# The norm's bias on the residual rows: sixteen half rows on GpSimd, or eight full rows on ScalarE inside the next projection

## The chip, the cores and the metric

The kernel runs on one core of a Trainium2 chip. The metric is the device time of one execution in microseconds; the median of three runs of the kernel before is 2121.49 us (2120.16 to 2122.59).

## What is computed

The reference is one inference step of a decoder trunk with two layers, for 512 prompt positions and 8 x 8 sample positions (576 columns in all) and a model width of 1024, in float32:

```python
for l in range(DEPTH):                      # DEPTH = 2
    mix, caches = token_mixer(x, ...)       # pooling, latent attention, gated MLP; from one projection w_in
    x = layernorm(ALPHA * x + mix, ln1_g[l], ln1_b[l])
    ffn, tail = conv_ffn(x, ...)            # w_up, 3-tap convolution, silu(gate) * up, w_down
    x = layernorm(ALPHA * x + ffn, ln2_g[l], ln2_b[l])

def layernorm(x, g, b):
    mu = mean(x); xc = x - mu
    return xc * rsqrt(mean(xc * xc) + LN_EPS) * g + b
```

So there are four norms, n = 0 to 3: two in layer 0 and two in layer 1. The result of a norm goes to two places: into the next projection, and, multiplied by ALPHA, into the next residual sum. The change is about the second.

## The kernel before

**Layout.** Features lie on the 128 partitions, positions in the free dimension. The residual X is a tile of eight rows (k = 0 to 7, one for each 128 features) of 576 columns. A half row is 288 of them. For TensorE every float32 operand is split into a high part (fp32r) and the remainder: X into XH and XL, a weight unit WS into WH (ScalarE copies, helper line 548) and WL (VectorE subtracts, line 1434). Each product takes three matmuls: WH XH, WH XL, WL XH. A tile of 128 output features takes 8 x 3 matmuls for one half of the columns and 48 for both (line 1010).

**Order.** There is no scheduler: each engine's program is written out by hand, and semaphores that only count up tie them together. Weight units (512 KB, or 704 KB for the down projection) are fetched by SP through two main slots; a slot's next fetch waits until VectorE has made the unit's remainder (w_lo). TensorE waits for w_lo and for the PSUM pair (mm_free0 or mm_free1) that ScalarE or VectorE releases once it has read it.

**A norm.** The projection before a norm (w_out or the second half of w_down) is done in two passes over the columns. While the second pass runs, the first half of the columns is normalised. The second half is normalised while TensorE already runs six tiles of the next projection on the first half (`first_halves`). The steps of a half, by line: VectorE centres (1451), ScalarE squares (574), TensorE sums through a matrix of ones (1052 to 1070), ScalarE takes the root (579), VectorE the reciprocal (1461) and then, for each row k, the scaled row X[k] = X[k] * gain * 1/sigma (1468, semaphore n_xn). ScalarE writes XH[k] = X[k] + bias (593, semaphore n_hi), and VectorE the remainder XL[k] = X[k] + bias - XH[k] (1479, semaphore n_lo). Both read X without the bias. So X itself gets the bias only after n_lo of its row: GpSimd does it, in `add_bias` (lines 491 to 495), one half row after another, and counts n_x. In the second half the order on ScalarE is: weight copy, XH rows 0 and 1, rows 2 to 4, the eviction of the fifth tile (which releases mm_free0), rows 5 to 7, the eviction of the sixth.

**After norms 0 and 2** comes the up projection: 11 tile pairs j = 0 to 10 in each of two halves hf, a gate tile (par 0) and an up tile (par 1) each. For j = 0, 2 and 4 of hf = 0 the six tiles of `first_halves` have already made the first half of the columns (kept in STASH), so that only 24 matmuls a tile are left; the other pairs take 48 a tile. In `up_tile` ScalarE copies the state (SFT) and the tile into EB, then makes a weight's high part, and for the gate tile runs silu when VectorE's convolution taps (1963, 1970, 1976) are done; last it copies HX to HH. The Silu table is loaded at line 938, ahead of j = 0. On VectorE a weight's remainder stands behind the taps of the gate tile (except for the half tiles, where it stands after the first tap), and for the up tile behind the product of silu and up. VectorE waits for n_x ahead of the first down projection (line 2006).

**After norm 1** comes layer 1's combined projection w_in: six tiles a of `first_halves` on the first half, then tiles m = 0 to 11, of which 0 to 4 and 10 have only the second half left (24 matmuls). For each m ScalarE waits for the tile, copies a weight's high part, evicts the tile into Z and releases its PSUM pair. Between the tiles it also loads w_uk, w_ukt and w_uv, and at m = 3 squares the v rows (line 691), which TensorE sums behind tile 4 (line 1041). X is overwritten by gathered cache pages during the attention, so after norm 1 the biased X is saved to x_save in DRAM by GpSimd's queue (line 513), in four transfers of 576 KB, each behind four of the adds. The first gather of layer 1 (line 535), into the space of X, waits for all four.

Norm 3 is the last; its bias is added by ScalarE on the way to the output, and nothing changes there.

Of the kernel before, what the change touches and what calls it, by code (L numbers as in the profile page):

```python
# [106 lines left out]
def build(nc, x_t, x_save, cache_wide, page_table, branch_in, w_uk, w_ukt, w_uv, state_ffn_t, params,  # L107
# [3 lines left out]
    with ctx:  # L111
# [353 lines left out]
        @block.gpsimd  # L465
        def _(pool):
            for name, n in CREDIT.items():
                pool.sem_inc(S[name], n)

            def norm(l, n, m0):  # L470

                def sum_up(half, k):
                    u = 8 * half + k
                    pool.wait_ge(S[f"mm_free{u % 2}"], CREDIT[f"mm_free{u % 2}"] + l * NM + m0 + u // 2 + 1)
                    if k == 0:
                        return
                    h = half_of(half)
                    pool.tensor_tensor(XS[:, h], X[:, 0, h] if k == 1 else XS[:, h], X[:, k, h], ALU.add)  # L478
                    ins = pool.drain()
                    if k == (DT - 1, DT - 2)[half]:  # L480
                        ins.then_inc(S["n_xs"], 1)

                def sum_squares(half, k):
                    pool.wait_ge(S["n_sq"], ln(n, half, k + 1))
                    h = half_of(half)
                    pool.tensor_tensor(SS[:, h], LSQ[:, 0, h] if k == 1 else SS[:, h], LSQ[:, k, h], ALU.add)
                    ins = pool.drain()
                    if k == (DT - 1, DT - 3)[half]:
                        ins.then_inc(S["n_sqs"], 1)

                def add_bias(half, k):
                    pool.wait_ge(S["n_lo"], ln(n + 1, half, k + 1))
                    h = half_of(half)
                    pool.tensor_scalar(X[:, k, h], X[:, k, h], param(l, (C_1B, C_2B)[n % 2] + k), None, ALU.add)\
                        .then_inc(S["n_x"], 1)

                last = n == 2 * DEPTH - 1
                for k in range(DT):
                    sum_up(0, k)
                for k in range(1, DT):  # L500
                    sum_squares(0, k)
                for k in range(DT - 1):
                    sum_up(1, k)
                if not last:
                    for k in range(1, DT - 2):
                        sum_squares(1, k)
                    for half in range(2):
                        for k in range(DT):
                            add_bias(half, k)
                            if n % 2 == 1 and k % 4 == 3:  # L510
                                pool.wait_ge(S["n_x"], ln(n, half, k + 1))
                                ks = slice(k - 3, k + 1)
                                pool.dma_start(x_save[:, ks, half_of(half)], X[:, ks, half_of(half)])\
                                    .then_inc(S["x_saved"], 16)

            for l in range(DEPTH):
                for u in range(NU2):
                    b, j = u // 4, u % 4
                    if u == 0 and l == 0:
                        pool.wait_ge(S["mask"], 1)  # L520
                        pool.wait_ge(S["n_lo"], ln(0, 1))
                    if u == 0 and l > 0:
                        pool.wait_ge(S["x_saved"], 64 * l)
                    if u == 1:
                        pool.wait_ge(S["mm_done0"], CREDIT["mm_done0"] + l * NM + M_UQ + 2)
                        pool.wait_ge(S["w_lo"], l * NU + U_UQ + 2)
                    if u == 2:
                        for other in ("met_pe", "met_act", "met_dve"):
                            pool.wait_ge(S[other], l * N_MEET + 1)
                    if u >= 4:  # L530
                        pool.wait_ge(S["pv_mm"], CREDIT["pv_mm"] + l * NU2 + u - 3)
                    past(pool)
                    for q in range(NQ):
                        g = b * NG + NQ * j + q
                        pool.indirect_dma_start(  # L535
                            raw_of(u)[:, q, :], None, cache_wide.rearrange("l n c -> (l n) c"),
                            bass.IndirectOffsetOnAxis(ap=IDXS[:, l, g:g + 1], axis=0))\
                            .then_inc(S[f"g_landed{u % 4}"], 16)
                for n in range(4):
                    pool.wait_ge(S[f"g_landed{n}"], 16 * NQ * landings(l, NU2 - 4 + n))  # L540
                past(pool)
                norm(l, 2 * l, M_OUT)
                norm(l, 2 * l + 1, M_DOWN[1])

        @block.scalar
        def _(act):
# [34 lines left out]
            def normal_hi(n, half, ks):  # L581
                h, b0 = half_of(half), (C_1B, C_2B)[n % 2]
                for k in ks:
                    if n < 0:
                        act.wait_ge(S["x_in_b"], 32)
                        copy(XH[:, k, h], X[:, k, h]).then_inc(S["x_hi"], 1)
                        continue
                    act.wait_ge(S["n_xn"], ln(n, half, k + 1))
                    if n == 2 * DEPTH - 1:
                        nc.scalar.activation(X[:, k, h], X[:, k, h], ACT.Identity,  # L590
                                             bias=param(n // 2, b0 + k)).then_inc(S["n_x"], 1)
                    else:
                        nc.scalar.activation(XH[:, k, h], X[:, k, h], ACT.Identity,
                                             bias=param(n // 2, b0 + k)).then_inc(S["n_hi"], 1)

            def half_passes(l, n, u0, m0, width):

# [53 lines left out]
            for l in range(DEPTH):  # L651
# [24 lines left out]
                for m in range(12):  # L676
# [4 lines left out]
                    if m < 11:  # L681
                        weight_hi(l * NU + U_IN + m + 2, D if m < 10 else QT * 384)
                        if z_of[m] is not None:
                            evict(m)
                            act.wait_ge(S["z_ev"], l * 16 + 6 + (m + 1 if m < 5 else m - 1))
                            act.sem_inc(S[f"mm_free{m % 2}"], 1)
                    if m == 3:
                        if l == 0:
                            act.wait_ge(S["params"], 16)
                        act.wait_ge(S["v_centred"], l + 1)  # L690
                        nc.scalar.activation(SQV[:, :, :], Z[:, 8:10, :], ACT.Square).then_inc(S["v_sq"], 1)
# [277 lines left out]
                for hf in range(2):  # L969
                    first = 2 * len(UP_FIRST) if hf == 0 else 0  # L970
                    for j in range(first):
                        up_tile(hf, j, D, UP_FIRST.index(j) if j in UP_FIRST else None)
                    with act.Fori(first, FH - 1) as j:
                        up_tile(hf, j, D)
                    up_tile(hf, FH - 1, UW, last=hf == 1)
# [1209 lines left out]
```

## Time and profile before

| | |
|---|---|
| median of the runs | 2121.49 us |
| profiled execution, first to last instruction (its only time) | 2123.8 us |
| TensorE matmul / weight load busy | 2047.8 / 1891.6 us |
| VectorE / ScalarE / GpSimd busy | 1194.9 / 804.0 / 401.2 us |
| mean granted TensorE clock | 0.994 |

Busy time is the time in which an engine had an instruction under way. An idle time in brackets behind a row is that of its engine just before the row, with what ended it. "Issue" there stands for a release that the profile does not show. In rows that merge several instructions, xN gives their number. Times in rows are microseconds from the start of the span, the mean duration in groups is in nanoseconds. The granted clock is given as a share of full speed; 1.00 is 2.4 GHz and 0.50 is 1.2 GHz.

### The profile page before, as it was taken

To read this page: it belongs to the slowest core of one execution; us is meant where nothing else is said; L and a number is where in the kernel's file an instruction comes from. 1 tells how busy PE (TensorE), PEld (TensorE's weight loads), DVE (VectorE), ACT (ScalarE), POOL (GpSimd) and SP (SyncE) were. 2 spreads that over 40 slices of the span, in tenths; PEclk is the share of its full clock that TensorE was granted. 3 is DMA by queue.
4 is the path that set the end of the run, shared out by engine and by line. 5 is a ranking of instruction groups with operands and counts; after the bars stand their busy time and mean duration, and the time that the engine had idled before them with its cause. 6 is when DMAs were issued, how large, how long until landed. Compare 5 with 4: busy or idle time off the path is not lost.

```text
span 2123.8 us, 43041 instructions
## 1 busy us (share of the span) xinstructions
PE 2047.8 (96%) x17374; PEld 1891.6 (89%) x17374; DVE 1194.9 (56%) x2032; ACT 804.0 (38%) x1508; POOL 401.2 (19%) x407
## 2 busy tenths in 40 slices
PE   7999999999998999999999999999999999999997
PEld 7976667999998999999989766689999889999997
DVE  4764545333578652666758644453335876436665
ACT  4343434222354321334443443342223543223334
POOL 0026661000051000000350366600002600000012
PEclk9999999999999999999999999999999999999999
DMA  7349996222433232225452599942225232222252
GB/s 253 118 149 328 373 353 232 80 79 80 156 108 96 84 105 67 79 79 181 136 206 68 174 364 365 370 161 88 80 79 175 90 100 79 99 71 82 79 195 73
DMA packets 88850, 325.69 MB, mean 153 GB/s; under 512 B 10576, under 2 KB 15568, under 8 KB 88592
## 3 DMA queue, kind: packets, MB, share of 16 engines
q1 hardware_dynamic: 46512, 169.52, 24.4%
q0 software_dynamic: 37440, 144.98, 18.4%
q10 hardware_dynamic: 4768, 9.37, 1.4%
q8 instruction: 92, 1.51, 0.3%
q14 instruction: 38, 0.31, 0.0%
HBM read 315.52 MB, written 7.26 MB: 152 GB/s over the span
## 4 chain that ended last, share of the span: by engine, by line
PE 84%; DVE 8%; ACT 3%; DMA 2%; issue 1%; DVEq 1%; POOL 0%; PEldq 0%; SPq 0%; ACTq 0%; PEld 0%; POOLq 0%
PE PS L1010 65%; PE PS L1292 5%; PE PS L1262 5%; DVE m_WL L1434 3%; PE PS L1283 2%; DMA m_WS<-in_w_units 1%; PE PS L1273 1%; ACT m_WH L548 1%; DVE m_X L1468 1%; PE PS L1315 1%; DVE m_XS L1479 1%; PE PS L1041 1%; PE PS L1331 1%; PE PS L1322 1%; PE PS L1309 1%
## 5 line engine op out<-in xcount | busy, mean ns | idle before, releaser
L1010 PE MATMUL PS<-m_XS,m_WH 128*128 128x288 f32 x5120 | 922.0, 297 | 34.6 <-DVE m_WL L1434 18.0
L1010 PEld LDWEIGHTS PS<-m_XS,m_WH 128*128 128x128 f32 x5120 | 767.9, 189 | 43.7 <-DVE m_WL L1434 20.9
L1010 PE MATMUL PS<-m_XS,m_WL 128*128 128x288 f32 x2560 | 583.5, 297 | 0.0
L1434 DVE TENSOR_TENSOR m_WL<-m_WS,m_WH 128x1024 fp32r<-128x1024 f32 (+2 forms) x284 | 369.2, 1301 | 229.9 <-ACT m_WH L548 221.0
L548 ACT ACTIVATE m_WH<-m_WS 128x1024 fp32r<-128x1024 f32 (+2 forms) x284 | 315.6, 1113 | 374.6 <-PE PS L1010 341.1
L1010 PEld LDWEIGHTS PS<-m_XS,m_WL 128*128 128x128 f32 x2560 | 423.5, 189 | 0.0
L535 POOL DMA_INDIRECT m_RAW<-in_cache_wide,m_IDXS x256 | 242.4, 947 | 380.2 <-PE PS L1010 124.4
L478 POOL TENSOR_TENSOR m_XS<-m_X 128x288 f32<-128x288 f32 x8 | 10.6, 1320 | 1170.5 <-DVE m_X L1488 1169.5
L1010 PE MATMUL PS<-m_HH,m_WH 128*128 128x288 f32 x704 | 205.7, 299 | 5.2 <-DVE m_X L1488 4.9
L1010 PE MATMUL PS<-m_HL,m_WH 128*128 128x288 f32 x704 | 203.5, 296 | 0.0
L1010 PE MATMUL PS<-m_HH,m_WL 128*128 128x288 f32 x704 | 180.3, 297 | 0.0
L1010 PEld LDWEIGHTS PS<-m_HH,m_WH 128*128 128x128 f32 x704 | 133.0, 189 | 6.3 <-DVE m_WL L1434 5.3
L1010 PEld LDWEIGHTS PS<-m_HL,m_WH 128*128 128x128 f32 x704 | 133.2, 189 | 0.2
L1292 PE MATMUL PS<-m_RAW,m_PT 128*64 128x256 f32 x1024 | 124.6, 385 | 7.4 <-ACT m_PT L548 7.1
L1262 PE MATMUL PS<-m_RAW,m_QSF 64*64 64x256 f32 x1024 | 125.3, 382 | 0.9 <-DMA m_RAW<-in_cache_wide,m_IDXS 0.9
L1262 PE MATMUL PS<-m_RAW,m_QSR 64*64 64x256 f32 x1024 | 124.4, 382 | 0.0
L1010 PEld LDWEIGHTS PS<-m_HH,m_WL 128*128 128x128 f32 x704 | 123.2, 189 | 0.0
L1963 DVE TENSOR_SCALAR m_CC<-m_EB,m_PARS 128x592 f32<-128x592 f32 x88 | 51.9, 590 | 123.5 <-ACT m_EB L548 123.4
L1292 PEld LDWEIGHTS PS<-m_RAW,m_PT 128*64 128x64 f32 x1024 | 67.8, 136 | 47.8 <-ACT m_PT L548 14.6
L902 ACT ACTIVATE m_SIG<-PS 128x576 f32<-128x576 f32 x48 | 31.2, 650 | 185.7 <-PE PS L1010 185.7
L1786 DVE TENSOR_SCALAR_CACHE_REDUCE PS<-PS,m_NMX 128x512 f32<-128x512 f32 x64 | 48.5, 759 | 92.0 <-PE PS L1273 92.0
L1262 PEld LDWEIGHTS PS<-m_RAW,m_QSF 64*64 64x64 f32 x1024 | 69.0, 133 | 28.0 <-issue 16.1
(276 smaller groups left out, 2875.4 us busy)
## 6 DMA issues: line engine op xcount, KB each, us to landing
m_WS<-in_w_units SPq DMA_DIRECT2D x232, 512.0 KB
m_WS<-in_w_units SPq DMA_DIRECT2D x48, 704.0 KB
m_RAW<-in_cache_wide,m_IDXS POOLq DMA_INDIRECT x256
m_X<-in_x_t SPq DMA_DIRECT2D x6, 576.0 KB, 7.4
m_WS<-in_w_units SPq DMA_DIRECT2D x4, 576.0 KB
x_save<-m_X POOLq DMA_DIRECT2D x4, 576.0 KB, 4.4
m_X<-x_save SPq DMA_DIRECT2D x4, 576.0 KB, 6.9
out_y<-m_X SPq DMA_DIRECT2D x8, 288.0 KB, 2.2
```

The lines of the kernel that those rows point to most:

```text
L535: pool.indirect_dma_start(raw_of(u)[:, q, :], None, cache_wide.rearrange("l n c -> (l n) c"), bass.IndirectOffsetOnAxis(ap=IDXS[:, l, g:g ...
L548: return nc.scalar.activation(out, in_, ACT.Copy)
L902: nc.scalar.activation(h2(SIG[:, g, :]), pair(g % 2), ACT.Sigmoid)\
L1010: mm = pe.matmul(out(half), w(part, k), x(k)[:, half_of(half)], start=(k == 0 and part == 0 and x is xh), stop=(k == last and part == 1))
L1041: mm = pe.matmul(PS[:, bank + h, 0:HT], C["ones"], x[:, h * HT:(h + 1) * HT], start=(k == 0), stop=(k == len(tiles) - 1))
L1262: pe.matmul(PS[64 * c:64 * c + 64, score_bank(u) + h, 0:256], weights, raw_of(u)[rows, c::2, at0:at0 + P], start=(g == 0), stop=False)
L1273: mm = pe.matmul(out[:, :, j, :], QSP[j][rows, rows_of], raw_of(u)[rows, c::2, 2 * KL:ROW], start=False, stop=(j == 1))
L1283: mm = pe.transpose(PS[:, 6, j * P:(j + 1) * P], PRB[:, j * P:(j + 1) * P], ident)
L1292: mm = pe.matmul(PS[64 * c:64 * c + 64, 7, 0:KL], PT[:, a, 64 * c:64 * c + 64], raw_of(u)[:, 2 * (a // 2) + c, j * KL:(j + 1) * KL], start ...
L1434: return dve.tensor_tensor(out, x, hi.bitcast(F32), ALU.subtract)
L1786: dve.tensor_scalar(s0, s0, -SCALE, NMX[:, b, j:j + 1], ALU.mult, ALU.min, accum_out=NMX[:, b, j + 1:j + 2]).then_inc(S["s_max"], 1)
L1963: dve.tensor_scalar(cc, e[:, 2:CV], tap(2), PARS[:, bass.ds(l * NPAR + C_CB + c, 1)], ALU.mult, ALU.add)
```

## The change

GpSimd's sixteen half-row adds of each of norms 0, 1 and 2 go. ScalarE adds the bias to eight full rows instead, as an Identity activation with the bias as its operand. It waits for the second half's n_lo of the row and counts n_x up by 2. After norms 0 and 2 it does rows 0 and 1 at the end of `up_tile` j = 2, rows 2 and 3 at the end of j = 3, and so on to j = 5. After norm 1 it does two rows at each of the tiles m = 0 to 3 of layer 1's combined projection, behind the eviction and the release of the PSUM pair. x_save is written in two transfers of 1152 KB, still from GpSimd's queue, each behind four full rows.

```diff
--- before.py
+++ after.py
@@ in gpsimd, norm() @@
-                def add_bias(half, k):
-                    pool.wait_ge(S["n_lo"], ln(n + 1, half, k + 1))
-                    h = half_of(half)
-                    pool.tensor_scalar(X[:, k, h], X[:, k, h], param(l, (C_1B, C_2B)[n % 2] + k), None, ALU.add)\
-                        .then_inc(S["n_x"], 1)
-
@@
-                    for half in range(2):
-                        for k in range(DT):
-                            add_bias(half, k)
-                            if n % 2 == 1 and k % 4 == 3:
-                                pool.wait_ge(S["n_x"], ln(n, half, k + 1))
-                                ks = slice(k - 3, k + 1)
-                                pool.dma_start(x_save[:, ks, half_of(half)], X[:, ks, half_of(half)])\
-                                    .then_inc(S["x_saved"], 16)
+                    if n % 2 == 1:
+                        for c in range(2):
+                            pool.wait_ge(S["n_x"], ln(n, 0, 0) + DT * (c + 1))
+                            ks = slice(4 * c, 4 * c + 4)
+                            pool.dma_start(x_save[:, ks, :], X[:, ks, :]).then_inc(S["x_saved"], 16)
@@
-                        pool.wait_ge(S["x_saved"], 64 * l)
+                        pool.wait_ge(S["x_saved"], 32 * l)
@@ in scalar @@
+            def add_bias(n, ks):
+                for k in ks:
+                    act.wait_ge(S["n_lo"], ln(n + 1, 1, k + 1))
+                    nc.scalar.activation(X[:, k, :], X[:, k, :], ACT.Identity,
+                                         bias=param(n // 2, (C_1B, C_2B)[n % 2] + k)).then_inc(S["n_x"], 2)
@@ in scalar, tiles m of the combined projection, behind the eviction @@
+                    if l > 0 and m < 4:
+                        add_bias(2 * l - 1, (2 * m, 2 * m + 1))
@@ in scalar, up projection @@
                     for j in range(first):
                         up_tile(hf, j, D, UP_FIRST.index(j) if j in UP_FIRST else None)
+                        if j >= 2:
+                            add_bias(2 * l, (2 * j - 4, 2 * j - 3))
```

## Rows read from the trace of the kernel before

**Rows 1.** The page, busy time, share of the span and instructions.
```profile
PE 2047.8 (96%) x17374; PEld 1891.6 (89%) x17374; DVE 1194.9 (56%) x2032; ACT 804.0 (38%) x1508; POOL 401.2 (19%) x407
```

**Rows 2.** The chain that ended last: the page's shares, and one piece in time.
```profile
PE 84%; DVE 8%; ACT 3%; DMA 2%; issue 1%; DVEq 1%; POOL 0%; PEldq 0%; SPq 0%; ACTq 0%; PEld 0%; POOLq 0%
...
644.42 16.12 PE PS L1010 x120
```

**Rows 3.** Timeline of TensorE: start, duration, instruction; in brackets idle before.
```profile
639.76 0.51 PE L1010 MATMUL PS<-m_XS,m_WH 128*128 128x288 f32 x2 [1.67 <-issue]
...
661.25 0.54 PE L1010 MATMUL PS<-m_XS,m_WH 128*128 128x288 f32 x2 [0.72 <-DVE m_WL L1434]
...
687.91 0.54 PE L1010 MATMUL PS<-m_XS,m_WH 128*128 128x288 f32 x2 [2.06 <-DVE m_WL L1434]
...
1082.94 0.82 PE L1010 MATMUL PS<-m_XS,m_WH 128*128 128x288 f32 x2 [3.59 <-issue]
```

**Rows 4.** Timeline of GpSimd at norms 0 and 1.
```profile
625.76 20.47 POOL L494 TENSOR_SCALAR m_X<-m_X,m_PARS 128x288 f32<-128x288 f32 x16 [0.22 <-issue]
...
1070.59 0.85 POOL L513 DMA_DIRECT2D x_save<-m_X  x1 [0.30 <-POOL m_X L494]
...
1085.05 4.80 POOL L494 TENSOR_SCALAR m_X<-m_X,m_PARS 128x288 f32<-128x288 f32 x4
```

**Rows 5.** Timeline of VectorE in the second half of norm 1.
```profile
1077.72 0.95 DVE L1479 SCALAR_TENSOR_TENSOR m_XS<-m_X,m_PARS,m_XS 128x288 fp32r<-128x288 f32 x2 [1.85 <-ACT m_XS L593]
...
1082.96 0.75 DVE L1479 SCALAR_TENSOR_TENSOR m_XS<-m_X,m_PARS,m_XS 128x288 fp32r<-128x288 f32 x1
...
1084.07 0.51 DVE L1479 SCALAR_TENSOR_TENSOR m_XS<-m_X,m_PARS,m_XS 128x288 fp32r<-128x288 f32 x1
```

**Rows 6.** Timeline of ScalarE, up projection of layer 0.
```profile
643.00 1.28 ACT L938 ACT_TABLE_LOAD   x1
...
677.50 0.20 ACT L548 ACTIVATE m_EB<-m_SFT 128x16 f32<-128x16 f32 x1
...
681.05 0.70 ACT L962 ACTIVATE m_SL<-m_CC 128x592 f32<-128x592 f32 x1 [1.81 <-DVEq L1979]
682.31 0.22 ACT L548 ACTIVATE m_EB<-m_SFT 128x16 f32<-128x16 f32 x1 [0.56 <-PE PS L1010]
...
687.35 0.20 ACT L548 ACTIVATE m_EB<-m_SFT 128x16 f32<-128x16 f32 x1
```

**Rows 7.** ScalarE's instructions by line: count, ns min/median/max, first and last start.
```profile
L702 ACT ACTIVATE m_Z<-m_Z,m_PARS x4: 852/854/857, 71.5 to 1123.6; 128x576 f32<-128x576 f32 x4
...
L593 ACT ACTIVATE m_XS<-m_X,m_PARS x48: 517/536/540, 605.9 to 1692.5; 128x288 fp32r<-128x288 f32 x48
```

**Rows 8.** Timeline of VectorE, weight remainders in the up projection.
```profile
681.10 1.23 DVE L1434 TENSOR_TENSOR m_WL<-m_WS,m_WH 128x1024 fp32r<-128x1024 f32 x1
...
702.93 1.22 DVE L1434 TENSOR_TENSOR m_WL<-m_WS,m_WH 128x1024 fp32r<-128x1024 f32 x1
```

**Rows 9.** Engines by stretch: length, busy each, granted clock, DMA share, GB/s.
```profile
688.00:692.00 4.00, 4.00 (x21) 4.00 (x22) 3.81 (x7) 1.18 (x3) 0.00 (x0) 0.63 0.53 147
...
1084.00:1088.00 4.00, 4.00 (x19) 4.00 (x18) 4.00 (x6) 1.37 (x3) 3.75 (x4) 0.50 0.44 155
...
1740.00:1744.00 4.00, 4.00 (x32) 4.00 (x32) 2.44 (x4) 1.41 (x6) 0.00 (x0) 1.00 0.64 229
```

**Rows 10.** The chain around norm 1: weight units, from request to landing.
```profile
1071.23 4.95 DMA m_WS<-in_w_units
...
1091.27 7.17 DMA m_WS<-in_w_units
```

**Rows 11.** Timelines of ScalarE and of TensorE: the v rows' square and its sum.
```profile
1102.26 1.17 ACT L691 ACTIVATE m_SQV<-m_Z 128x1152 f32<-128x1152 f32 x1
...
1104.22 2.10 PE L1041 MATMUL PS<-m_SQV,m_CST 128*128 128x288 f32 x8
```

## The prediction

> **What bounds the kernel now.** I read the page's engine shares first, then its chain, then TensorE's gaps in order of time, and last the queues of VectorE, ScalarE and GpSimd around the three places where the bias is added. The shares show a kernel that TensorE bounds nearly everywhere [rows 1], and the chain says the same; it holds stretches of 120 matmuls in 16.12 us, 0.134 us each [rows 2]. So a change on other engines counts only where TensorE stands still, or where it is made to. The reader is to see in [rows 3] that it stands still around every norm: 1.67 us at 639.76 and 0.72 at 661.25 behind norm 0, 2.06 at 687.91 in the up-projection, 3.59 at 1082.94 behind norm 1. Norm 2 repeats norm 0, 1050.3 us later. I call the up tiles j0, j1, ..., each a gate half (p0) and an up half (p1).
>
> GpSimd adds the sixteen half rows in one run, 20.47 us at norm 0, and at norm 1 in pieces between the x_save transfers, to 1089.85 [rows 4]. In just that time VectorE does the second half of the norm.
>
> **Part 1, sixteen adds leave GpSimd.** VectorE's remainder rows (L1479) show a price for them. At norm 1 one took 0.75 us while GpSimd worked, and the next one 0.51, while GpSimd, whose next adds start at 1085.05, was issuing a transfer [rows 4, 5]. So an overlapping add costs a remainder row 0.24 us. I take it from six remainder rows, and guess 0.34 in all for the scaled rows in the stretch: 1.8 us at norm 0 and again at norm 2, of which 1.5 lies before the last scaled row. Bounds: 0 (the slow ones are slow for another reason) and 16 x 0.24 = 3.8.
>
> The Trainium skill (SBUF — State Buffer, "Who interferes with whom") says that a VectorE instruction with two SBUF inputs contends with a GpSimd one that reads SBUF, and that one of the two blocks fully. Both VectorE forms here have two SBUF inputs; by that rule all sixteen would gain, 3.8 us, where the rows show a part of it. The sum goes by the rows.
>
> At norms 0 and 2 the last scaled row gates ScalarE's XH row 7, the sixth stash and then the table load, 1.28 us from 643.00 [rows 6]; they move 1.5 us earlier, and j0's copies with them. j0 and j1 are paced by ScalarE and VectorE (the 0.72 us gap at 661.25 ends on VectorE's weight split), so j2 starts 1.5 us earlier too: shift -1.5.
>
> **Part 2, eight full rows on ScalarE in j2 to j5 (norms 0 and 2).** A full row with a bias is not in this form in the trace. Below: the half row with a bias, 0.536 us; above: the full row with bias and scale, 0.854 [rows 7]. A pair costs 1.07 to 1.71; I take 1.35, a little under the middle, since rows in a row overlap. The Trainium skill (ScalarE: Activation LUTs, "What ACT_TABLE_LOAD costs") gives 280 ns + 0.833 ns per element for an activation with a bias operand and 93 ns of overlap; an estimate from that is 1.33 for a pair.
>
> The pair stands behind j's HH copy, ahead of the next tile's copies. Queued behind it: the copies of the gate half, behind these VectorE's taps and its weight split, and TensorE waits for the split.
> - After j2: ScalarE starts j3's copies at 677.50 with nothing idle before [rows 6]. New start: 677.50 - 1.5 + 1.35 = 677.35. The split for j4p0 ends 4.83 us later (681.10 + 1.23 - 677.50) [rows 8], at 682.2. TensorE, 1.5 us early, wants it at 680.8 (before, it came without a gap at 682.3): a new gap of 1.4 us.
> - j3p1's copies: ScalarE waited 0.56 us for TensorE there, to 682.31. Now silu is last, at 681.05 + 0.70 - 0.15, less 0.1 of overlap, 681.5: shift -0.8, and the split that ended the 2.06 us gap also comes 0.8 early, at 687.1.
> - After j3: 687.35 - 0.8 + 1.35 = 687.9, shift +0.55, carried rigidly through j4, where ScalarE never waits for TensorE. j5p0's weights come 0.7 us late for TensorE, which loses nothing more in the end, as the next line sets the time.
> - After j4: shift +0.55 + 1.35 = +1.9 at j5's copies. The split for j6p0 ended at 704.15 [rows 8]; now at 706.05. TensorE would be there at 687.1 + 0.7 + 16.1 (120 matmuls of 0.134) = 703.95: a gap of 2.1 us.
> - After j5: the pair ends before j6p0 does (6.4 us of TensorE); from here on TensorE bounds again, and nothing gives the delay back. VectorE's wait for n_x ahead of the first down projection costs nothing: the last pair ends near 712, and five more tile pairs of 12.9 us (j6 to j10) hide it.
>
> Before, TensorE began j6p0 16.1 us after 687.91 at norm 2's place (704.05), and 1.5 us later at norm 0, where the clock fell: 21 matmuls in four microseconds at 0.63 against 32 at 1.00 for the like tiles behind norm 2, 11 x 0.134 = 1.5 [rows 9]. So norm 0 costs +0.5 and norm 2 +2.0: +2.5. The shift at j5 is 2b - 0.8 with its own part of b in 0.8; with b from 1.07 to 1.71 the two together give +0.8 to +4.7.
>
> The clock: the same 2.06 us gap dropped it to 1.2 GHz at norm 0 and not at norm 2. The new 2.1 us gaps at j6p0 are of that size, one behind each norm. Half of them at 1.5 us, and a little for j4: +1.7 (bounds 0 and 3.5). Part 2 with what part 1 gives to it: **+4.2 us**.
>
> **Part 3, norm 1.** Two things end together: GpSimd's adds, and the four x_save transfers in the middle of the second half (one issued at 1070.59) [rows 4]. The weight unit requested at 1071.23 took 4.95 us to land and VectorE stood still for 1.85 us behind it [rows 5, 10], with its 512 KB beside a transfer of 576. Its share of the bytes is 2.3 us, the lower bound; I take 3.2. That gives 1.8 us, the scaled and remainder rows another 0.6 up to row 4, whose XH copy is ahead of the eviction that frees the PSUM pair: TensorE starts at about 1080.55, not 1082.94: -2.4. Its gap was 3.59 us and put the clock at 0.50: 19 matmuls in four microseconds, not 32, is 1.7 us [rows 9], and with what that stretch leaves out on both sides I take 2.3. The new gap is 1.6, like that of 639.76, behind which 120 matmuls ran at full pace [rows 2]. -4.7. The next tile's split waits for the last remainder row: +0.6.
>
> Then the pairs come, in tiles of half length (3.2 us): each 1.35 us behind the eviction and its release, so TensorE's tiles go on. Late is what ScalarE does after them: the square for v at 1102.26, which had its result 0.8 us before TensorE summed it at 1104.22 [rows 11]. Now the weight of tile 5 at 1096.0 (1.06), its eviction (0.3), the last pair (1.35) and the square (1.17) end at 1099.9, where TensorE would be at 1099.2. Net at this sum: 1104.3 - 1099.9 = **-4.4 us** (bounds -2.5 and -5.9, TensorE's own pace). Behind it full tiles of 6.4 us cover ScalarE. GpSimd's second transfer, twice the size, starts at about 1099, 9 us behind its last adds before, and the first gathers follow it; six such tiles and the whole query stage lie between them and the attention that reads them.
>
> **Sum.** +4.2 - 4.4 = -0.2. The page gives 2123.8 us as the span and no other time for its execution; the runs' median is 2121.49, 0.1% under it, so the difference is carried over: **2121.3 us**.
>
> **Rivals.**
> - *The pairs are hidden in the up-projection.* ScalarE is busy for 38% of the span only [rows 1], and the gap of 0.56 us before 682.31 is some cover. Against it: no idle time stands before 677.50 and 687.35 [rows 6], and the split at 681.10 is just in time. If so: -1.5 twice, -4.4: -7.4, 2114.1.
> - *The new x_save transfer delays a weight unit* (the other side). It is issued by GpSimd at about 1091.5, with the fetch for tile 5. A fetch at 1091.27 took 7.17 us among other transfers [rows 10]. At that price the unit lands at 1098.9, the square is done at 1102.8, TensorE waits 3.6 us and the clock falls as it did at 1082.94, 2.3 us: norm 1 gives +0.7 instead of -4.4, total +4.9: 2126.4. It decides from a landing of some 6.5 us on. Against it: 3.2 us of the seven were three loads that are over by then.
> - *GpSimd is not what slows VectorE.* Then -1.5 twice and 1.0 at norm 1 are missing: +3.8, 2125.3. Against it speaks 0.51 beside 0.75 [rows 5].
> - *Identity under the Silu table needs a load.* Each pair would cost two loads of 1.28 us in eight places, +20: 2142. Copies run there without one; no row has Identity there. The Trainium skill (ScalarE: Activation LUTs, "Table sets: the hidden batching unit") has identity in every set.
>
> **How the numbers follow.** Forecast 0.52 (its own range 2118 to 2124.5), hidden pairs 0.17, late weights 0.15, no contention 0.08, table loads 0.03, something else 0.05. Two tenths of a per cent is 4.2 us, about what can be told from no change. Faster: 0.17 and 0.05 of the forecast's edge, 0.22. Slower: 0.14, 0.03 and 0.03: 0.20. Same: 0.58. The range takes in the hidden pairs and the late weights: 2114 to 2127.
>
> **What the changed profile would show.** Right: remainder rows of 0.51 us in all three second halves; no gap over 2 us at the start of layer 1's tile 0 and the clock at 1.00 there; new gaps before j4p0 (1.4 us) and j6p0 (2.1 us), ended by VectorE's split; Identity rows near 0.77 us. Wrong: j4p0 and j6p0 without gaps (hidden), a fetch over 6 us behind the first x_save (late weights), remainder rows of 0.75 with GpSimd idle (no contention), or a clock that falls behind each new gap.

## The result and the profile after

The changed kernel takes 2125.9 us (median of 19 runs, 2122.46 to 2130.76), the kernel before on the same chip 2122.59 us (19 runs): ratio 1.0016, 95% interval 1.0009 to 1.0024, some 3.4 us slower. The forecast was 2121.3 us, 0.2 under before. So its time lies in the range, and the direction is wrong by a small but clear amount. The runs of one kernel spread by 8 us and more, which is more than the effect; a single profiled span (2122.0 us here) therefore says nothing on a total, and below traces are compared piece by piece.

TensorE's gaps in the changed kernel, from its timeline (start, duration, instruction, idle before). Helper lines have moved: 1010 is 1011, 1434 is 1435, 1479 is 1480, 548 is 539.

```profile
637.05 0.51 PE L1011 MATMUL PS<-m_XS,m_WH 128*128 128x288 f32 x2 [0.85 <-issue]
...
662.73 0.54 PE L1011 MATMUL PS<-m_XS,m_WH 128*128 128x288 f32 x2 [1.63 <-DVE m_WL L1435]
...
680.27 0.54 PE L1011 MATMUL PS<-m_XS,m_WH 128*128 128x288 f32 x2 [1.43 <-DVE m_WL L1435]
685.13 0.54 PE L1011 MATMUL PS<-m_XS,m_WH 128*128 128x288 f32 x2 [1.39 <-DVE m_WL L1435]
689.04 0.80 PE L1011 MATMUL PS<-m_XS,m_WH 128*128 128x288 f32 x4 [0.44 <-DVE m_WL L1435]
...
704.08 1.32 PE L1011 MATMUL PS<-m_XS,m_WH 128*128 128x288 f32 x4 [2.29 <-DVE m_WL L1435]
...
1082.33 0.56 PE L1011 MATMUL PS<-m_XS,m_WH 128*128 128x288 f32 x2 [1.99 <-issue]
...
1102.93 2.21 PE L1042 MATMUL PS<-m_SQV,m_CST 128*128 128x288 f32 x8 [0.92 <-ACT m_SQV L690]
...
1755.13 1.32 PE L1011 MATMUL PS<-m_XS,m_WH 128*128 128x288 f32 x4 [2.13 <-DVE m_WL L1435]
```

Against [rows 3] the gap of 1.67 us behind norm 0 has become 0.85, and the one of 3.59 behind norm 1 has become 1.99. The gap of 1.63 at 662.73 was there before (1.45). Four are new: 1.43 us before j4p0 (680.27), 0.44 before j5p0 (689.04), 2.29 before j6p0 (704.08; 2.13 at 1755.13 in layer 1), and 0.92 before the sum of the v squares. The gap that was 2.06 before j4p1 is 1.39 (685.13).

ScalarE's instructions by line, and two pieces of VectorE's timeline in the second half of norm 1:

```profile
L590 ACT ACTIVATE m_X<-m_X,m_PARS x24: 758/762/779, 674.1 to 1760.0; 128x576 f32<-128x576 f32 x24
```
```profile
1077.52 0.95 DVE L1480 SCALAR_TENSOR_TENSOR m_XS<-m_X,m_PARS,m_XS 128x288 fp32r<-128x288 f32 x2 [0.99 <-ACT m_XS L584]
...
1080.38 0.51 DVE L1480 SCALAR_TENSOR_TENSOR m_XS<-m_X,m_PARS,m_XS 128x288 fp32r<-128x288 f32 x1
```

The full row takes 0.762 us, between the two of [rows 7]. The remainder rows take 0.51 us, not 0.75 [rows 5].

The engines by stretch behind the new gaps (columns as in [rows 9]), and the chain of waits at norm 1:

```profile
704.00:708.00 4.00, 3.92 (x19) 3.93 (x20) 3.58 (x8) 1.31 (x3) 0.00 (x0) 0.60 0.40 131
708.00:712.00 4.00, 4.00 (x32) 4.00 (x32) 1.47 (x2) 1.72 (x3) 0.00 (x0) 1.00 0.42 126
1080.00:1084.00 4.00, 2.01 (x11) 1.81 (x10) 4.00 (x10) 1.98 (x5) 0.00 (x0) 0.83 0.39 133
1084.00:1088.00 4.00, 4.00 (x25) 4.00 (x24) 1.97 (x3) 1.44 (x3) 0.00 (x0) 0.74 0.45 123
...
1756.00:1760.00 4.00, 4.00 (x23) 4.00 (x23) 3.83 (x7) 1.31 (x3) 0.00 (x0) 0.69 0.38 131
```
```profile
1072.61 3.37 DMA m_WS<-in_w_units
1080.47 1.86 issue
1082.33 11.35 PE PS L1011 x72
1093.68 1.94 PE PS L1042 x8
1095.62 3.21 PE PS L1011 x24
1102.93 2.21 PE PS L1042 x8
```

In this execution the granted clock fell to 1.2 GHz behind all three gaps: the four microseconds from 704 hold 19 matmuls, those from 708 hold 32. The weight unit landed in 3.37 us, where it took 4.95 [rows 10]. Behind it 72 matmuls took 11.35 us, which at 0.134 us each would be 9.65.

**Three lengths.** The pieces compared lie between waits that every version has. *Norm 1* runs from TensorE's wait for the second half's square sum to its wait for the v product: 1067.79 to 1146.31 before, 1069.17 to 1144.88 after. *To j6* runs from the wait for the first half's sum (614.15 after) to j6p0. With late pairs j6p0 has no gap of its own, and the start of j4p1 is read instead (*to j4p1*).

| | before | after | difference | predicted |
|---|---|---|---|---|
| to j6, layer 0 | 89.51 | 89.93 | +0.4 | +0.5 |
| to j6, layer 1 | 87.98 | 89.96 | +2.0 | +2.0 |
| low clock behind j6p0 | in neither | in both layers | +3.0 | +1.7 |
| norm 1 | 78.52 | 75.71 | -2.8 | -4.4 |

At 704.08 the first 12 matmuls took 3.04 us where 12 x 0.134 is 1.61, so a drop costs 1.4 to 1.5 us. The sum is +2.6, inside the 1.9 to 5.1 us of the ratio.

The row on the clock holds for this execution only. Here are the windows behind j6p0 of a second execution of the changed kernel (layer 0, j6p0 at 703.73 behind a gap of 2.14 us) and of *norms 0 and 2 alone* (layer 1, j6p0 at 1757.03, gap 2.13):

```profile
704.00:708.00 4.00, 4.00 (x32) 4.00 (x32) 3.76 (x8) 1.31 (x3) 0.00 (x0) 1.00 0.41 131
```
```profile
1756.00:1760.00 4.00, 2.97 (x22) 2.98 (x23) 3.53 (x7) 1.96 (x5) 0.00 (x0) 1.00 0.39 131
```

The clock stayed up at both. Four profiled executions have this gap, 1.9 to 2.3 us long, once in each layer, and the clock fell behind 6 of the 8. At 1.5 us each that makes +2.3 on the average, not +3.0. The second execution has 76.06 us at norm 1, -2.5. With both the sum is +2.2.

### The profile page after: what moved, and what is told of

Its sections match the earlier page's. It is cut to its first block, busy times and chain, and to the rows that moved or that the text cites. A ratio compares the mean times of both kernels' runs of the same rounds, so it can differ in the third digit from the quotient of the medians.

```text
span 2122.0 us, 43039 instructions
## 1 busy us (share of the span) xinstructions
PE 2044.8 (96%) x17374; PEld 1889.1 (89%) x17374; DVE 1189.1 (56%) x2032; ACT 819.7 (39%) x1532; POOL 337.8 (16%) x357
## 3 DMA queue, kind: packets, MB, share of 16 engines
q8 instruction: 92, 1.51, 0.3%
## 4 chain that ended last, share of the span: by engine, by line
PE 81%; DVE 9%; ACT 4%; DMA 2%; issue 2%; DVEq 1%; POOL 1%; PEldq 0%; SPq 0%; ACTq 0%; PEld 0%; POOLq 0%
PE PS L1011 62%; PE PS L1293 5%; PE PS L1263 5%; DVE m_WL L1435 3%; PE PS L1284 2%; ACT m_WH L539 1%; PE PS L1274 1%; DMA m_RAW<-in_cache_wide,m_IDXS 1%; DVE m_X L1469 1%; PE PS L1042 1%; PE PS L1316 1%; DMA m_WS<-in_w_units 1%; DVE m_CC L1977 1%; PE PS L1332 1%; DVE m_XS L1480 1%
```

## The experiments

The versions were measured in three groups; those of one group share a chip and its runs of the kernel before, whose medians were 2120.73 us (*norm 1 alone*, *norms 0 and 2 alone*, *late pairs*, *no adds*), 2119.67 (*late pairs at all three norms*, *GpSimd adds, but later*, *x_save alone*, *fill before j6*) and 2122.66 (the other four). The diffs show the lines that matter; removed lines and the changed counts of x_saved are left out where the text tells them.

### The two halves of the change by themselves

**Norm 1 alone.** ScalarE adds at m = 0 to 3 as in the changed kernel; after norms 0 and 2 GpSimd adds as before.

```diff
+                    if n % 2 == 0:
+                        for half in range(2):
+                            for k in range(DT):
+                                add_bias(half, k)
```

> Only norm 1's adds are on ScalarE; norms 0 and 2 keep GpSimd's half rows. Theory A (the adds in the up projection are what costs; the clock fell behind the new gaps): only norm 1's gain is left, 1.5 to 3 us below the kernel before. Theory B (the loss is at norm 1, from the late x_save transfers and the later square): slower than before by 1 to 3 us. The trace should show norm 1's stretch, from the sum of squares to the v product near 1146, 2.8 us shorter than before, as in the changed kernel.

Measured: 2119.82 us, ratio 0.9993 [0.9981, 1.0005]: -1.5 us, not told from nothing. Norm 1 takes 76.05 us, 2.5 less than before, with the same gaps as in the changed kernel.

**Norms 0 and 2 alone.** The pairs in the up projection as in the changed kernel; norm 1 and x_save as before.

> Only norms 0 and 2 have their adds on ScalarE. Theory A: slower than before by 4 to 7 us (2.4 us of gaps, and 1.5 us of low clock behind each gap of 2.1 to 2.3 us at j6p0). Theory B: within 1 us of the kernel before or faster. Gaps expected at j4p0 1.4, j4p1 1.4, j6p0 2.2 us.

Measured: 2128.14 us, ratio 1.0029 [1.0017, 1.0040]: +6.1 us (3.6 to 8.5). To j6 it is 89.94 and 89.97 us, as in the changed kernel. So the loss is in the up projection. The predicted +4.2 is within the interval, and so are 4.8 (0.5 + 2.0 + 2.3 for the clock) and the 5.5 of two drops: the time doesn't tell them apart.

### Is it the place of the pairs?

**Late pairs.** Two rows each behind j = 6 to 9 instead of 2 to 5.

```diff
-                        if j >= 2:
-                            add_bias(2 * l, (2 * j - 4, 2 * j - 3))
+                    if hf == 0:
+                        for j in range(first, FH - 1):
+                            up_tile(hf, j, D)
+                            add_bias(2 * l, (2 * j - 12, 2 * j - 11))
```

> The pairs stand behind the tiles j = 6 to 9 instead of j = 2 to 5, all else as in the changed kernel. Theory A: no new gap at j4p0 and j6p0; the 1.5 us that the earlier start gives stay, at norms 0 and 2; 5 to 7 us below the changed kernel, 2 to 4 below the one before. Rival (ScalarE has no 1.35 us to spare in j6 to j9 either, its idle time there being 1.4 to 3 us a pair of tiles): no better than the changed kernel.

Measured: 2113.82 us, ratio 0.9964 [0.9952, 0.9976], 7.6 us faster than before and so 11 faster than the changed kernel: more than the 2 to 4 and 5 to 7 that were expected. The gaps before j4p0, j5p0 and j6p0 are gone. The gap of 2.1 us stands before j4p1 again. The pieces named so far give 5.4 (1.5 at each of norms 0 and 2, 2.4 at norm 1); the last section has a difference in TensorE's pace that may be the rest.

**No adds at all.** ScalarE counts n_x up and adds nothing: the residual's bias after norms 0 to 2 is left out of the result.

```diff
-                    nc.scalar.activation(X[:, k, :], X[:, k, :], ACT.Identity,
-                                         bias=...).then_inc(S["n_x"], 2)
+                    act.sem_inc(S["n_x"], 2)
```

> Leaves the bias on the residual rows out altogether (ScalarE only counts the semaphore up at the same places), so the residual sums lack it. It bounds what any placement can give. Theory A: 1.5 us at each of norms 0 and 2, 4 to 6 us at norm 1: 7 to 9 us below the kernel before. If GpSimd's adds do not slow VectorE: 3 to 5 us, with remainder rows of 0.75 us remaining in the second halves.

Measured: 2118.24 us, ratio 0.9984 [0.9972, 0.9997], only 3.4 us faster than before, not the 7 to 9 expected, although nothing is left to add. So it isn't the lower bound of the change that it looks like: the median of the late pairs is 4.4 us lower (the two intervals just touch, at 0.9972 to 0.9976). Norm 1 takes 76.79 us, more than the changed kernel, although the clock did not fall there. This version's chain of waits:

```profile
1079.79 5.66 DMA m_WS<-in_w_units
1087.88 6.41 DMA m_WS<-in_w_units
1097.23 2.21 PE PS L1041 x8
```

Two weight units land in 5.66 and 6.41 us and TensorE waits 1.74 us for the v square behind them. The first lands beside ScalarE's loads of w_ukt and w_uk. The second was requested at 1087.88, and GpSimd had issued the first x_save transfer, 1152 KB, at 1087.34: this is the rival *late weights*, in a version that it was not predicted for. So at norm 1 it is not ScalarE's pairs alone that limit.

**Late pairs at all three norms.** The late pairs of above, and at norm 1 at m = 5 to 8 instead of 0 to 3.

```diff
-                    if l > 0 and m < 4:
-                        add_bias(2 * l - 1, (2 * m, 2 * m + 1))
+                    if l > 0 and 5 <= m < 9:
+                        add_bias(2 * l - 1, (2 * m - 10, 2 * m - 9))
```

> As late_j, and norm 1's pairs stand at the full tiles m = 5 to 8 instead of m = 0 to 3, with the x_save transfers behind them. If the x_save transfer among the short tiles is what holds norm 1's gain at 2.7 us: the fetches of tiles 4 and 5 land in 5 us or less and the wait for the square (0.92 us) goes; 1 to 3 us below late_j. If the clock behind the gap at tile 0 holds it: the same as late_j within 1 us.

Measured: 2111.99 us, ratio 0.9968 [0.9956, 0.9981], not told from the 0.9964 of the late pairs. Norm 1 takes 74.88 us, 0.8 less than in the changed kernel, and the wait for the v square is gone. Pairs and transfers moved together here, so this doesn't say which of them ended the wait. TensorE's timeline in the up projection:

```profile
637.55 0.50 PE L1014 MATMUL PS<-m_XS,m_WH 128*128 128x288 f32 x2 [0.85 <-issue]
...
663.22 0.53 PE L1014 MATMUL PS<-m_XS,m_WH 128*128 128x288 f32 x2 [1.61 <-DVE m_WL L1438]
684.98 0.54 PE L1014 MATMUL PS<-m_XS,m_WH 128*128 128x288 f32 x2 [2.08 <-DVE m_WL L1438]
```

From 614.64 to j4p1 at 684.98 it is 70.34 us; before it was 687.91 - 616.04 = 71.87 [rows 3]. That is 1.53 us less with no pair on the way: part 1's shift of 1.5, by itself.

**The same once more**, in the third group.

> The pairs behind j = 6 to 9 and, at norm 1, behind m = 5 to 8, once more. If the gain is real it repeats: 6 to 8 us under the kernel before, ratio 0.9962 to 0.9975.

Measured: 2110.04 us (6 runs), ratio 0.9946 [0.9927, 0.9965]: faster than expected. The two intervals share 0.9956 to 0.9965, which is 7.4 to 9.3 us under the kernel before. No version has a lower median, but the late pairs alone (0.9964) aren't told from it.

### Is it GpSimd's overlap, and what of x_save?

**GpSimd adds, but later.** The kernel before, with GpSimd's adds held back: after norms 0 and 2 behind six tile pairs, at norm 1 behind the last n_lo, and x_save in two transfers behind them.

```diff
+                    if n % 2 == 0:
+                        pool.wait_ge(S["h_lo"], l * 2 * FH + 6)
                     for half in range(2):
                         for k in range(DT):
+                            if n % 2 == 1 and k == half == 0:
+                                pool.wait_ge(S["n_lo"], ln(n + 1, 1))
                             add_bias(half, k)
```

> GpSimd keeps the adds, but starts them behind the norm: after norms 0 and 2 when six tile pairs of the up projection are done, after norm 1 when the whole remainder is written, and saves x_save in two transfers behind them. If GpSimd's adds cost only by overlapping the second half of the norm, this has the early starts (gaps of 0.85 us, not 1.67, remainder rows of 0.51) without ScalarE's work in j2 to j5: 5 to 8 us below the kernel before, as late_j. If an add slows VectorE's taps in the steady up projection enough to delay TensorE: gaps there, and 0 to 3 us below only.

Measured: 2115.9 us, ratio 0.9983 [0.9972, 0.9994], 3.6 us faster (1.3 to 5.9) with the same adds on the same engine, where 5 to 8 were expected. VectorE's timeline at norm 0, with GpSimd idle until 707.47:

```profile
635.69 0.51 DVE L1483 SCALAR_TENSOR_TENSOR m_XS<-m_X,m_PARS,m_XS 128x288 fp32r<-128x288 f32 x1
636.12 0.51 DVE L1472 SCALAR_TENSOR_TENSOR m_X<-m_X,m_PARS,m_RN 128x288 f32<-128x288 f32 x1
636.55 0.51 DVE L1483 SCALAR_TENSOR_TENSOR m_XS<-m_X,m_PARS,m_XS 128x288 fp32r<-128x288 f32 x1
```

The same rows of the kernel before, while GpSimd adds from 625.76 [rows 4]:

```profile
637.69 0.67 DVE L1479 SCALAR_TENSOR_TENSOR m_XS<-m_X,m_PARS,m_XS 128x288 fp32r<-128x288 f32 x1
638.29 0.50 DVE L1468 SCALAR_TENSOR_TENSOR m_X<-m_X,m_PARS,m_RN 128x288 f32<-128x288 f32 x1
638.72 0.75 DVE L1479 SCALAR_TENSOR_TENSOR m_XS<-m_X,m_PARS,m_XS 128x288 fp32r<-128x288 f32 x1
```

The engine that adds is the same, only the time differs, so it is GpSimd's overlapping adds that slow VectorE, by 0.16 to 0.24 us a single remainder row; the single scaled rows between them take 0.50 and 0.51 either way. Over the whole second half of norm 0, six of the eight remainder rows are slowed, 1.3 us in all, and of the scaled rows two, which took 0.69 and 0.76 us: 0.4 more. The Trainium skill (SBUF — State Buffer, "Who interferes with whom") would have one of the two engines block fully, 3.8 us over the sixteen rows by the prediction's estimate; the traces show 1.7 us in the rows and the 1.53 us above in TensorE's start. The rival *GpSimd is not what slows VectorE* falls.

At norm 1 this version has the shortest stretch of all, 74.37 us. The gap before tile 0 and the window behind it:

```profile
1078.59 0.50 PE L1014 MATMUL PS<-m_XS,m_WH 128*128 128x288 f32 x2 [2.09 <-issue]
```
```profile
1080.00:1084.00 4.00, 3.56 (x27) 3.32 (x26) 2.82 (x5) 2.19 (x4) 2.62 (x2) 1.00 0.35 98
```

The clock stayed at 1.00 behind a gap of 2.09 us. By its pieces this version should gain some 7 us (1.56 and 1.51 up to j4p1 in the two layers, 4.1 at norm 1), and its TensorE waits nowhere in the up projection while GpSimd adds. Why the runs show 3.6 only stays open.

**x_save alone.** The kernel before, with x_save in two transfers of 1152 KB behind all sixteen adds.

```diff
+                    if n % 2 == 1:
+                        pool.wait_ge(S["n_x"], ln(n, 1))
+                        for c in range(2):
+                            ks = slice(4 * c, 4 * c + 4)
+                            pool.dma_start(x_save[:, ks, :], X[:, ks, :]).then_inc(S["x_saved"], 16)
```

> The kernel before with one change: the x_save transfers are issued behind all sixteen adds (two of 1152 KB), so none is in flight with the weight unit of the second half. If the transfers made most of norm 1's stall: that unit lands in 3.4 us instead of 4.95 and tile 0 starts 1.5 to 2 us earlier, gap near 2.2 us; 1 to 3 us below the kernel before. If GpSimd's adds made it: under 1 us of gain, gap near 3 us.

Measured: 2119.62 us, ratio 1.0004 [0.9996, 1.0013]. The gap before tile 0 shrinks from 3.59 to 2.44 us, and tile 0 starts 1.5 us earlier in the stretch (13.62 us behind its start, 15.15 before). So of the 2.0 us that the changed kernel gains up to there (13.16), the transfers of x_save are 1.5 and GpSimd's adds the rest. Here it is given back at once; TensorE's gaps and the chain:

```profile
1089.17 2.21 PE L1041 MATMUL PS<-m_Z,m_CST 128*128 128x288 f32 x8 [0.79 <-ACT m_Z L548]
...
1097.00 0.53 PE L1010 MATMUL PS<-m_XS,m_WH 128*128 128x288 f32 x2 [2.44 <-DVE m_WL L1434]
```
```profile
1084.44 10.10 DMA m_WS<-in_w_units
```

A weight unit takes 10.10 us beside the big transfers, and norm 1 takes 80.50 us, 2.0 more than before. This is the mechanism of the rival *late weights* in a version in which x_save goes out 5.5 and 12 us earlier in the stretch than in the changed kernel. There the transfers are issued at 1094.94 and 1102.14, behind three and behind all five of the half tiles m = 0 to 4, and TensorE has no wait behind a weight unit from then on.

### Is it the clock?

**Fill before j6.** The changed kernel with 14 more matmuls, results unread, in TensorE's gap before j6p0.

```diff
+                    if hf == 0:
+                        for f in range(14):
+                            pe.matmul(PS[:, 4, 0:HT], XH[:, 0, 0:P], XH[:, 0, 0:HT], start=True, stop=True)
                     with pe.Fori(first, FH) as j:
```

> The changed kernel with 14 matmuls (1.9 us) whose results nobody reads put in front of j6p0, where TensorE waits 2.2 us for the weight remainder anyway. If the clock that falls behind that gap costs 1.5 us at each of norms 0 and 2: no low clock near 704 and 1756 and 1 to 3 us below the changed kernel. If the low clock there is of no weight: the same time, within 0.7 us.

Measured: 2120.01 us, ratio 1.0001 [0.9987, 1.0014]. The windows of this version:

```profile
704.00:708.00 4.00, 3.71 (x29) 3.49 (x28) 3.49 (x7) 2.35 (x5) 0.00 (x0) 1.00 0.27 78
1756.00:1760.00 4.00, 4.00 (x32) 4.00 (x31) 3.28 (x5) 2.02 (x3) 0.00 (x0) 1.00 0.27 81
```

The clock stays at 2.4 GHz in both layers, and the ratio is 3 to 4 us under the changed kernel's, where 2.3 to 3.0 would be the drops. The intervals overlap a little, so the time supports the price and does not prove it; the windows show the clock up, behind a gap at which it fell 6 times in 8 without the fill.

**The changed kernel again, and with a fill before tile 0 of layer 1.** Both in the third group.

```diff
                 first_halves(l, 2 * l - 1, U_INA, M_INA, (l - 1, M_DOWN[1]))
+                if l > 0:
+                    for f in range(14):
+                        pe.matmul(PS[:, 4, 0:HT], XH[:, 0, 0:P], XH[:, 0, 0:HT], start=True, stop=True)
```

> The changed kernel once more, so that the two fills can be read against it on one chip. Every theory expects 2 to 4 us above the kernel before (ratio 1.0008 to 1.0020), with the same gaps to 0.1 us: 1.4 before j4p0, 2.2 before j6p0, 2.0 before tile 0 of layer 1, 0.9 before the sum of the v squares.

> The changed kernel with 14 matmuls, unread, in TensorE's gap ahead of tile 0 of layer 1's combined projection. Theory A (the low clock behind that gap costs what it seems to, 1.7 us, and nothing else limits the stretch): granted clock 1.00 there, the stretch from the last square sum to the v product falls from 75.7 to about 74.1 us, time 1.5 us under the changed kernel. Theory B (the slow clock only hides that ScalarE's chain of adds, weight copies and the v square is the limit): the clock stays at 1.00, but TensorE's wait for the v square grows from 0.9 to about 2.5 us, the stretch stays at 75.7, and the time is that of the changed kernel. Theory C (the weights' landings cap it, as in the version without adds): new waits of TensorE for a weight's remainder in tiles 1 to 4, the stretch 75 to 76.

Measured: the changed kernel 2125.51 us, 1.0018 [1.0003, 1.0032], as in the first measurement. With the fill 2125.59 us, 1.0014 [1.0001, 1.0028]: the same. Norm 1 takes 76.06 us in both. The windows, TensorE's gaps and the chain with the fill:

```profile
1084.00:1088.00 4.00, 3.56 (x26) 3.33 (x26) 3.46 (x7) 2.15 (x5) 0.00 (x0) 1.00 0.31 107
```
```profile
1087.69 0.54 PE L1011 MATMUL PS<-m_XS,m_WH 128*128 128x288 f32 x2 [0.44 <-DVE m_WL L1438]
...
1094.91 2.21 PE L1042 MATMUL PS<-m_Z,m_CST 128*128 128x288 f32 x8 [0.55 <-ACT m_Z L539]
...
1104.43 2.21 PE L1042 MATMUL PS<-m_SQV,m_CST 128*128 128x288 f32 x8 [0.92 <-ACT m_SQV L690]
```
```profile
1085.98 0.52 DVE m_XS L1483
1086.50 1.15 DVE m_WL L1438
1087.65 0.02 issue
...
1087.76 5.72 DMA m_WS<-in_w_units
```

The clock no longer falls, and yet nothing is gained. Tile 0 starts 13.24 us after the start of the stretch in both (1083.81 - 1070.57, and 1080.86 - 1067.62 without the fill). The first three half tiles and the wait behind them then take 11.10 us, not 11.36; the v sum takes 2.21 us, not 1.94; and tile 3 starts after 26.55 us, not 26.54. TensorE now waits at two places which the low clock had covered. The 0.44 us before tile 1 is VectorE's: the split stands behind the norm's last remainder row. This is the +0.6 of the prediction. The 0.55 us before the v sum is behind the unit that took 5.72 us, beside ScalarE's loads of w_ukt and w_uk. The changed kernel has that late unit too, and ScalarE waits for it (requested at 1086.27, so 5.4 us):

```profile
1091.67 1.06 ACT L539 ACTIVATE m_WH<-m_WS 128x1024 fp32r<-128x1024 f32 x1 [1.38 <-DMA m_WS<-in_w_units]
```

So the third theory, that the weights' landings cap the stretch, fits in part; the norm's own end is the other part. The second does not: the wait for the v square stayed at 0.92 us, as it follows TensorE's own tile by a fixed chain on ScalarE (weight copy 1.06, eviction 0.39, pair 1.45, square 1.15) against a tile of 3.2 us.

**Late pairs with both fills.**

> The version with late pairs, with 14 unread matmuls each in the 2.1 us gap of the up projection (hf = 0, ahead of j = 6; in this version the gap lies earlier, ahead of j = 4's up tile, so that the fill there has no gap to fill and costs 14 x 0.134 = 1.9 us in each layer) and ahead of tile 0 of layer 1's combined projection (gain 1.5 us if the clock's price is real). Clock theory: +1.9 twice, -1.5 once: 2 us above the late version. If the fill at tile 0 gives nothing: 4 us above it.

Measured: 2115.1 us, ratio 0.9967 [0.9955, 0.9979], 5.1 us above the version without the fills, where 4 was expected if the fill at tile 0 gives nothing. Norm 1 takes 74.94 us against 75.04 without: nothing gained by the clock here either, with waits of 0.44 and 0.72 us behind it. The fills in the up projection, where this version has no gap, cost their own 1.9 us a layer, by their count. The most that a clock at 1.00 has gone with at norm 1 is 0.5 to 0.7 us, the 74.37 of GpSimd's late adds against 74.88 and 75.04: there the same unit landed in 5.2 us, and TensorE's second wait was under 0.2.

## Why the prediction was wrong

**Right, by its steps.** Part 1: an overlapping GpSimd add costs a remainder row 0.24 us, six of eight rows are slowed and the scaled rows by 0.4 (0.34 was the guess), and the half tiles start 1.5 us earlier (1.53 with late pairs). Part 2's pair: 1.35 us taken, 1.43 to 1.45 measured (start shift 1.34); gaps predicted 1.4, 0.7 and 2.1 us, measured 1.43, 0.44 and 2.29; up to j6p0 +0.5 and +2.0, measured +0.42 and +1.98. Part 3's landing: 3.2 taken, 3.37 measured. The pairs delay nothing outside the places named, and the Identity needs no table load (20 loads before and after).

**The step that failed: the clock at norm 1, and what was taken to stand behind it.**
- *"The new gap is 1.6, like that of 639.76, behind which 120 matmuls ran at full pace"*, with *2.3 us* for the drop gone. Tile 0 started 2.0 us earlier, not 2.4; its gap was 1.99 us, 2.07 in the second execution, and the clock fell in both. The drop cost 1.7 us; it had cost 2.5 before (the first 23 matmuls from 1082.94 took 5.6 us, 3.1 at 0.134 each). So 0.8 us came back, not 2.3.
- *The weights of tiles 1 to 4 as early enough.* The prediction let ScalarE's chain alone set the end, with 0.7 us of wait for the v square (0.92 measured, and behind a TensorE that was itself late). With the clock held up the stretch is no shorter: VectorE's split for tile 1, and a weight unit of 5.7 us (5.4 in the changed kernel) beside ScalarE's loads, take what the clock gives. So the 2.3 us were not there to be had. The term was -4.4 and measured -2.8 and -2.5: 1.6 to 1.9 us of the miss.
- *"Half of them at 1.5 us"* at j6p0. In the profiled execution both gaps dropped the clock: +3.0 in place of +1.7, 1.3 us. Over the four executions that have the gap it was 6 of 8, 0.6 us of the miss. With so few gaps a half is not ruled out, so this step was too low in this execution and is not shown wrong in the mean.

Together they make +2 to +3 us out of the predicted -0.2; measured is +3.4, interval 1.9 to 5.1. One sum of the prediction doesn't close either: with its own -2.4, -2.3 and +0.6 TensorE would be at 1100.2, not at 1099.2, and norm 1 would give -4.1.

**The rivals.** Hidden pairs: no, four new gaps. Late weights: not by x_save in the changed kernel, though by x_save in two other versions (6.41 and 10.10 us); the late unit of the changed kernel lands beside ScalarE's loads of w_ukt and w_uk, issued at 1085.12 and 1085.49. No contention and table loads: no.

**What the change gives and where it goes.** Taking GpSimd's adds from under VectorE's norm is worth 1.5 us at norms 0 and 2 each, and with x_save out of the way 3.5 us at norm 1 (74.88 and 75.04 with late pairs against 78.52): 6.5 in all, where the late pairs at all norms measured 6.8 and 11.5 (ratios 0.9968 and 0.9946). The changed kernel gives it up at norms 0 and 2, as it puts 1.45 us a pair in just the four tile pairs in which ScalarE and VectorE pace TensorE. Four tile pairs later the same instructions leave no gap.

## What to carry to other kernels

Work that is moved to a half-idle engine should be put where that engine has slack in time, and not where the data first allow it: ScalarE is busy for 39% of the changed kernel's span, and still paces TensorE in its half-length tiles. Where a gap of some 2 us in TensorE's work comes or goes, price the clock from both sides and by more than one execution, and then ask what is the second limit of the stretch, before the whole drop is booked as a gain. And adds on GpSimd cost less when VectorE isn't on the critical path, which a single wait can arrange (3.6 us here).

## What the hardware showed beside this

TensorE has more than one pace at the granted clock of 1.00. In the projections the start-to-start time of a 128x288 matmul is about 132 ns in some stretches and 134.4 in others, and it switches in the middle of a projection. The engines in one stretch of the up projection, first with late pairs at all norms, then in its repetition, the identical kernel:

```profile
760.00:820.00 60.00, 60.00 (x458) 60.00 (x457) 23.58 (x27) 12.70 (x13) 0.00 (x0) 1.00 0.28 95
```
```profile
760.00:820.00 60.00, 60.00 (x449) 60.00 (x448) 22.22 (x27) 12.94 (x13) 0.00 (x0) 1.00 0.28 94
```

With TensorE busy throughout and the clock at 1.00 in both, 60 us hold 458 matmuls in one and 449 in the other: 131 and 134 ns each. From the first half's sum to the second pass of w_down in layer 0 the same kernel took 372.58 us (987.22 - 614.64) in one execution and 376.00 (989.78 - 613.78) in the other, 3.4 us, as much as the whole effect of the change; a clock drop of 1.5 us behind the second of these marks lies in neither. In its profiled execution the version without adds had the slow pace from 740 on (375.23 us), the late pairs the fast one to 850 (372.85): 2.4 us of the 6.5 between these two executions. Of the 14 profiled executions, three of the four with late pairs have 458 matmuls in this stretch and the fourth 449; *x_save alone* has 463, and the other nine have 448 or 449. So part of what the late pairs gain may be the pace and not the gaps. What switches it stays open, and none of the versions tests it.

The clock behind gaps of 2.0 to 2.5 us isn't decided by the gap alone: it fell behind 6 of 8 gaps before j6p0 and, of the ten executions with 2.0 to 2.5 us before tile 0 of layer 1, in eight; the 2.5 us gap ahead of the second pass of w_down in layer 1 left the clock at 1.00 in one execution of the changed kernel and dropped it to 0.66 in the other (2040 to 2044), and the 2.1 us gap of [rows 3] dropped it in layer 0 only.
